# The S5 recurrence kept in PSUM, and the order of GpSimd's and ScalarE's work around it, in an encoder block on one Trainium2 core

## The chip, the core and the metric

The kernel runs on one core of a Trainium2 chip. The time is the device time of one execution in microseconds, as the median of several runs. The engines are TensorE (PE, with its weight loads as PEld), VectorE (DVE), ScalarE (ACT), GpSimd (POOL) and SyncE (SP), which here only issues DMAs. "arena" is one large tensor in SBUF that holds every buffer, "ps" is PSUM, eight banks of 512 float32 numbers in each of 128 partitions.

## What is computed

One layer of a bidirectional encoder for 512 tokens of width 1024, all in float32: a projection, a Mamba-2 branch (SSD), an S5 branch, gates, a layer norm, and a mixture of 16 experts. The change touches the S5 branch. Cut to it, the reference is:

```python
def _s5_direction(ug, a_re, a_im, log_step, b_re, b_im):
    lam = lax.complex(a_re, a_im)
    step = jnp.exp(log_step)[:, None]
    a_bar = jnp.exp(lam * step)
    b_bar = ((a_bar - 1.0) / lam)[..., None] * lax.complex(b_re, b_im)
    bu = jnp.einsum('blgk,gpk->blgp', ug.astype(jnp.complex64), b_bar)
    ...
    _, states = lax.associative_scan(combine, (a_seq, bu), axis=1)
    return states

def _s5_branch(u, ...):
    s_f = _s5_direction(ug, ..._f); s_b = flip(_s5_direction(flip(ug), ..._b))
    y = jnp.real(jnp.einsum('blgp,gkp->blgk', s_f + s_b, c))
    y = jax.nn.gelu(y + u * d_skip)
    return (y @ w_glu_a) * jax.nn.sigmoid(y @ w_glu_b)
```

## The kernel before

**Rounds.** The 48 groups of the S5 branch are packed in 24 pairs, and the pairs are worked through in six rounds of four (NQ = 6, QB = 4). A sequence of 512 is cut into 128 chunks of 4 tokens, so that a recurrence runs over 128 chunks, once forward (d = 0) and once backward (d = 1). The complex factor of the recurrence is split into modulus and phase: the input F is turned by a table of cosines and sines, a real scan with the modulus runs over it, and the result is turned back. The order is written out by hand; every wait is a semaphore.

**VectorE** does in round q: `maps(q + 1)`, the output maps `vc` of the next round (L1511 to L1515, then v_ready); `toeplitz_rows(q)` (L1641 to L1644); and `recur(q, 0)`, `recur(q, 1)` (L1648 to L1680). A recurrence reads F, which TensorE has put into PSUM banks 0 to 3, in four products with the tables (L1657 to L1660), adds them into zr and zi in SBUF (L1661, L1662, then F_read), runs eight scans, two for each pair (L1666, L1667), and turns the result into X with four products and two sums (L1673 to L1678, then X_ready).

**TensorE** does in round q: `toeplitz(q)`, 16 small products; `states(q)`, transposed input maps times U, which give F; `outputs(q - 1)`, which reads X of the round before and gives y5_ps; and three fills, each a tile of 128 x 512 of the gate projections. They are the tiles t = 2 to 4 in round 0, 5 to 7 in round 1 and so on, in the PSUM banks 4 and 7 by turns (`fill_bank`). The states wait for F_read of both directions of the round before, the outputs for X_ready. A fill waits until the one before the last has been drained (gate_copied).

**GpSimd** makes the tables. `tables(q, d)` (L529 to L535) waits for X_ready of the same direction one round before, whose tables it overwrites. `state_maps(q + 1)` (L492 to L501) makes the input maps `wc` of the next round; it stands between the two tables of round q and waits for in_ready, ScalarE's copy of the maps of the round before.

**ScalarE** does in round q: the copies of the Toeplitz products and of the four transposed maps, `gelu(q - 1)` (waits for y5_ps), `input_blocks(q + 1)` (eight copies, waits for w_ready of the state maps), and the drains of the three fills, with `output_blocks(q + 1)` behind the first. A drain is a sigmoid into the one buffer gstage and a DMA to gate_scratch; the next drain waits until that has landed.

**SyncE** stores and reloads the Toeplitz blocks and the outputs y5, and loads the projection weights in slices of 2 MB.

Of the kernel before, what the change touches and what calls it, by code (L numbers as in the profile page):

```python
# [24 lines left out]
ALU = mybir.AluOpType  # L25
# [137 lines left out]
def encoder(nc, A, out):  # L163
# [21 lines left out]
    with ExitStack() as ctx:  # L185
# [142 lines left out]
        toep_ps toep_copied toep_built toep_stored toep_loaded wT_ps wT_copied F_ps F_read par_ready conv_tap sel_built  # L328
# [176 lines left out]
        def _(pool):  # L505
# [64 lines left out]
            powers(coarse, FINE.bit_length() - 1)  # L570
            for q in range(NQ):
                for d in range(2):
                    tables(q, d)
                    pool.wait_ge(s.tab_ready, 2 * q + d + 1)
                    if d == 0 and q + 1 < NQ:
                        maps_tmp = pool_tmp.rearrange("p a b -> p (a b)").rearrange("p (i c) -> p i c", i=4)
                        state_maps(pool, n, [maps_tmp[:, i, :] for i in range(4)], q + 1)
# [28 lines left out]
        def _(act):  # L606
# [123 lines left out]
            for q in range(NQ):  # L730
                toeplitz_copied(q)
                for j in range(QB):
                    i = QB * q + j
                    act.wait_ge(s.wT_ps, i + 1)
                    if i >= 2:
                        act.wait_ge(s.F_ps, i - 1)
                    f(wT[:, i % 2].rearrange("p a b -> p (a b)"), ps[:, 5 + i % 2, :], ACT.Copy).then_inc(s.wT_copied, 1)
                if q >= 1:
                    gelu(q - 1)
                if q + 1 < NQ:  # L740
                    input_blocks(q + 1)
                for t in range(fills_before[q], fills_before[q + 1]):
                    (gate if t < GATES else first_channels)(t, fill_bank(t))
                    if t == fills_before[q] and q + 1 < NQ:
                        output_blocks(q + 1)
# [14 lines left out]
            for b in range(1, XBC // 512 + 1):  # L760
                for j in range(4):
                    i = 4 * b + j
                    if i < 20:
                        act.wait_ge(s.xbc_ps, i - 3)
                        if b == 1:
                            act.wait_ge(s.toep_loaded, 16 * 2 * T * NQ)
                            act.wait_ge(s.F_read, 2 * NQ)
                        else:
                            act.wait_ge(s.conv_done, 4 * b)
# [173 lines left out]
        def _(pe):  # L943
# [105 lines left out]
            def states(q):  # L1049
                pe.wait_ge(s.in_ready, q + 1)  # L1050
                pe.wait_ge(s.u_loaded, 16 * 2 * T)
                if q >= 1:
                    pe.wait_ge(s.F_read, 2 * q)
# [45 lines left out]
            for b in range(1, XBC // 512 + 1):  # L1099
                if b < XBC // 512:  # L1100
                    w = slice_wait()
                    for j in range(4):
                        i = 4 * b + j
                        if i == 6:
                            pe.wait_ge(s.F_read, 2 * NQ)
# [364 lines left out]
        def _(dve):  # L1470
# [175 lines left out]
            def recur(q, d):  # L1646
# [6 lines left out]
                if d == 1:  # L1653
                    F = [x[:, :, ::-1] for x in F]
                c, sn = cos_t[:, d], sin_t[:, d]
                flat = lambda x: x.rearrange("p g c -> p (g c)")
                tt(zr, F[0], c, ALU.mult)  # L1657
                tt(zi, F[1], c, ALU.mult)
                tt(t1, F[1], sn, ALU.mult)
                n.link(tt(t2, F[0], sn, ALU.mult))  # L1660
                tt(zr, zr, t1, ALU.add)  # L1661
                tt(zi, zi, t2, ALU.subtract).then_inc(s.F_read, 1)  # L1662
                dve.wait_ge(s.F_read, 2 * q + d + 1)
                for g in range(QB):
                    decay = modulus[:, d, QB * q + g:QB * q + g + 1].to_broadcast([P, NC])
                    n.done(dve.tensor_tensor_scan(t1[:, g], decay, zr[:, g], 0.0, ALU.mult, ALU.add))  # L1666
                    n.done(dve.tensor_tensor_scan(t2[:, g], decay, zi[:, g], 0.0, ALU.mult, ALU.add))  # L1667
# [5 lines left out]
                n.done(tt(o[0], e(t1), e(c), ALU.mult))  # L1673
                n.done(tt(o[1], e(t1), e(sn), ALU.mult))
                n.done(tt(zr, t2, sn, ALU.mult))
                n.link(tt(zi, t2, c, ALU.mult))
                tt(o[0], o[0], e(zr), ALU.subtract)
                ins = tt(o[1], o[1], e(zi), ALU.add)  # L1678
                ins.then_inc(s.X_ready, 1)
# [299 lines left out]
```

## Time and profile before

| | |
|---|---|
| median of 3 runs | 2209.75 us (2207.89 to 2210.27) |
| the profiled execution, its own time | 2202.2 us |
| its span | 2200.5 us |
| busy over the span | PE 1983.0 us (90%), PEld 943.1 (43%), DVE 648.4 (29%), ACT 381.4 (17%), POOL 237.3 (11%) |
| mean granted TensorE clock | 0.951 of full speed |
| 0 to 89 us | transposes, projections, the parameters of the S5 branch |
| 89 to 320 us | the six S5 rounds |
| 320 to 820 us | conv, SSD branch, gates and mixing |
| 820 us to the end | layer norm, router, experts; DMA share 0.96 |

Busy time of an engine is the time in which an instruction of it runs. The share over the span says little here, since the stages have different limits; the section after the next shows rows of the S5 rounds alone. A row of the timeline gives start, length, engine, line, operation, output and inputs with their shapes, and in brackets the idle time before it with the engine that ended it. Queued instructions overlap a little, so that a row's length can be more than the distance to the next start.

### The profile page before, as it was taken

What the parts mean: (1) busy time and instruction counts of PE and PEld (TensorE: products, weight loads), DVE (VectorE), ACT (ScalarE), POOL (GpSimd) and SP (SyncE); (2) the same over time, 40 slices, a digit from 0 to 9 for tenths busy, and PEclk for the clock granted to TensorE, in tenths of its full rate; (3) what the DMA queues carried; (4) which work ended last, traced back from release to release, by engine and by line L of the source; (5) the groups of instructions that cost most, each with busy time, mean ns of one, the idle gap of its engine ahead of it and who ended that gap; (6) DMA issues with size and microseconds to landing.
All of it is one profiled execution on the core that took longest, in us unless ns stands there. A gap on an engine that the chain in (4) does not pass through costs nothing.

```text
span 2200.5 us, 19980 instructions
## 1 busy us (share of the span) xinstructions
PE 1983.0 (90%) x8382; PEld 943.1 (43%) x8382; DVE 648.4 (29%) x1101; ACT 381.4 (17%) x684; POOL 237.3 (11%) x238
## 2 busy tenths in 40 slices
PE   8887899999989999799989888988988888988987
PEld 4555554456654445434334334333333333333332
DVE  6599977477750113400100100100100100100102
ACT  1433312257760002100001000000000000000001
POOL 1767520032210000000000000000000000000001
PEclk9898999999989999899989999999989999999989
DMA  5621222101113228699999999999999999999995
GB/s 141 125 73 64 69 58 81 67 29 45 42 58 134 86 72 353 257 421 425 427 428 428 427 427 428 427 427 428 428 426 428 428 427 426 429 426 427 429 427 225
DMA packets 88074, 625.49 MB, mean 284 GB/s; under 512 B 21180, under 2 KB 34736, under 8 KB 57776
## 3 DMA queue, kind: packets, MB, share of 16 engines
q1 hardware_dynamic: 75552, 616.41, 68.4%
q10 hardware_dynamic: 12432, 7.79, 1.2%
q8 instruction: 67, 1.10, 0.2%
q14 instruction: 23, 0.19, 0.0%
HBM read 614.39 MB, written 9.78 MB: 284 GB/s over the span
## 4 chain that ended last, share of the span: by engine, by line
PE 56%; DMA 27%; DVE 4%; ACT 1%; issue 1%; POOL 0%; SPq 0%; DVEq 0%; POOLq 0%
PE ps L945 54%; DMA arena<-in_w_e 27%; ACT arena L610 1%; DVE arena L1864 0%; DVE arena L1862 0%; DVE arena L1792 0%; PE ps L1396 0%; DVE arena L1955 0%; DVE arena L1912 0%; DVE arena L1666 0%; DVE arena L1667 0%; PE ps L1430 0%; PE ps L1120 0%; DVE arena L1753 0%; DVE arena L1949 0%
## 5 line engine op out<-in xcount | busy, mean ns | idle before, releaser
L945 PE MATMUL ps<-arena 128*64 128x512 f32 (+6 forms) x7850 | 1917.8, 529 | 186.6 <-DMA arena<-in_w_e 113.5
L945 PEld LDWEIGHTS ps<-arena 128*64 128x64 f32 (+2 forms) x7850 | 880.2, 164 | 1199.3 <-issue 1044.5
L610 ACT ACTIVATE arena<-ps 128x512 f32<-128x512 f32 (+5 forms) x292 | 164.7, 595 | 1684.5 <-PE ps L945 979.7
L1921 DVE TENSOR_TENSOR arena<-arena,ps 128x512 f32<-128x512 f32 (+1 forms) x48 | 30.2, 644 | 568.3 <-PE ps L945 568.2
L602 POOL TENSOR_TENSOR arena<-arena 128x1024 f32<-128x1024 f32 x3 | 7.1, 2351 | 1364.5 <-ACT arena L610 1364.5
L1930 DVE TENSOR_TENSOR arena<-arena,ps 128x512 f32<-128x512 f32 x48 | 33.1, 690 | 341.3 <-PE ps L945 341.3
L610 ACT ACTIVATE arena<-arena 128x128 f32<-128x128 f32 (+8 forms) x250 | 110.1, 503 | 78.2 <-DVE arena L1828 20.8
L610 ACT ACT_TABLE_LOAD x74 | 94.9, 1283 | 25.4 <-issue 23.7
L1712 DVE SCALAR_TENSOR_TENSOR arena<-arena 128x512 f32<-128x512 f32 x80 | 60.2, 753 | 2.8
L1912 DVE TENSOR_TENSOR arena<-arena 128x512 f32<-128x512 f32 x8 | 5.6, 694 | 179.2 <-PE ps L1430 179.2
L1511 DVE TENSOR_TENSOR arena<-arena 128x320 f32<-128x320 f32 x48 | 38.7, 865 | 0.4
L590 POOL TENSOR_TENSOR arena<-arena 128x768 f32<-128x768 f32 x16 | 24.4, 1524 | 101.2 <-PE ps L945 101.2
L492 POOL TENSOR_TENSOR arena<-arena 128x256 f32<-128x256 f32 x40 | 31.8, 826 | 1.1
L1667 DVE TENSOR_TENSOR_SCAN arena<-arena 128x128 f32<-128x128 f32 x48 | 31.8, 663 | 0.0
L1666 DVE TENSOR_TENSOR_SCAN arena<-arena 128x128 f32<-128x128 f32 x48 | 31.5, 655 | 0.4
L1810 DVE TENSOR_TENSOR arena<-ps,arena 128x512 f32<-128x512 f32 x8 | 5.5, 690 | 74.9 <-PE ps L945 39.1
L1818 DVE TENSOR_TENSOR arena<-ps,arena 128x512 f32<-128x512 f32 x8 | 5.5, 692 | 71.0 <-PE ps L945 71.0
L529 POOL TENSOR_TENSOR arena<-arena 128x512 f32<-128x512 f32 (+4 forms) x19 | 17.6, 926 | 67.6 <-DVE arena L1678 66.8
L591 POOL TENSOR_TENSOR arena<-arena 128x768 f32<-128x768 f32 x16 | 24.9, 1554 | 0.0
L587 POOL TENSOR_TENSOR arena<-arena 128x512 f32<-128x512 f32 x4 | 5.6, 1404 | 168.7 <-ACT arena L610 148.0
L1396 PE MATMUL ps<-arena 128*128 128x128 f32 x176 | 23.4, 289 | 0.0
L1396 PEld LDWEIGHTS ps<-arena 128*128 128x128 f32 x176 | 21.9, 211 | 3.1 <-DVE arena L1921 3.1
(192 smaller groups left out, 685.1 us busy)
## 6 DMA issues: line engine op xcount, KB each, us to landing
arena<-in_w_e SPq DMA_DIRECT2D x120, 2816.0 KB, 28.9
arena<-in_w_e SPq DMA_DIRECT2D x80, 2048.0 KB, 28.1
arena<-in_w_e SPq DMA_DIRECT2D x16, 1408.0 KB, 21.3
arena<-in_w_in SPq DMA_DIRECT2D x9, 2048.0 KB, 8.8
arena<-in_w_e SPq DMA_DIRECT2D x16, 1024.0 KB, 29.8
arena<-in_w_in SPq DMA_DIRECT2D x5, 1536.0 KB, 6.3
arena<-in_w_out_ssd SPq DMA_DIRECT2D x4, 1536.0 KB, 6.7
gate_scratch<-arena ACTq DMA_DIRECT2D x16, 256.0 KB, 2.9
```

Of the source, the lines that this page charges most:

```text
L492: n.done(eng.tensor_tensor(tmp[t], x, y, ALU.mult))
L590: pool.tensor_tensor(rhs_f, first(m_le, HG), last(da[:, c, f], P), ALU.mult)
L591: pool.tensor_tensor(rhs_b, first(m_ge, HG), last(da[:, c, b], P), ALU.mult).then_inc(s.mats_ready, 1)
L610: return act.activation(out, in_, func, **kw)
L945: return pe.matmul(out, lhsT, rhs, start=a, stop=z)
L1396: r = pe.transpose(ps[:, i, P * t:P * t + P], block[:, t, :], ident)
L1511: n.done(tt(tv[t], x, y, ALU.mult))
L1666: n.done(dve.tensor_tensor_scan(t1[:, g], decay, zr[:, g], 0.0, ALU.mult, ALU.add))
L1667: n.done(dve.tensor_tensor_scan(t2[:, g], decay, zi[:, g], 0.0, ALU.mult, ALU.add))
L1712: r = stt(cacc[:, j], raw[:, j, k:k + SEQ], conv_w[:, i, k:k + 1], cacc[:, j], ALU.mult, ALU.add)
L1921: tt(o, o, ps[:, i, 0:w], ALU.mult).then_inc(s.hid_ready, 1)
L1930: r = tt(o, o, ps[:, 6 + k % 2, :], ALU.add)
```

## The change

Four things are changed. The recurrence works in place in the PSUM banks of F: the two products with the sine go to t1 and t2 in SBUF, the rest is written over F, the scans run on F, and only X is in SBUF; F_read is gone, and what waited for it (the states, ScalarE's first copies of the conv input, the last outputs) waits for X_ready. GpSimd's backward table of round q waits for the output maps of round q + 1 (v_ready), and the state maps are made behind both tables, for round q + 2 (round 0 makes those of rounds 1 and 2). ScalarE's input blocks stand ahead of GELU.

```diff
@@ gpsimd
+            maps_tmp = pool_tmp.rearrange("p a b -> p (a b)").rearrange("p (i c) -> p i c", i=4)
             for q in range(NQ):
                 for d in range(2):
+                    if d == 1 and q + 1 < NQ:
+                        pool.wait_ge(s.v_ready, q + 2)
                     tables(q, d)
                     pool.wait_ge(s.tab_ready, 2 * q + d + 1)
-                    if d == 0 and q + 1 < NQ:
-                        maps_tmp = pool_tmp.rearrange("p a b -> p (a b)").rearrange("p (i c) -> p i c", i=4)
-                        state_maps(pool, n, [maps_tmp[:, i, :] for i in range(4)], q + 1)
+                for q_ in ([1] if q == 0 else []) + ([q + 2] if q + 2 < NQ else []):
+                    state_maps(pool, n, [maps_tmp[:, i, :] for i in range(4)], q_)
@@ scalar
+                if q + 1 < NQ:
+                    input_blocks(q + 1)
                 if q >= 1:
                     gelu(q - 1)
-                if q + 1 < NQ:
-                    input_blocks(q + 1)
...
-                            act.wait_ge(s.F_read, 2 * NQ)
+                            act.wait_ge(s.X_ready, 2 * NQ)
@@ tensor, states
                 if q >= 1:
-                    pe.wait_ge(s.F_read, 2 * q)
+                    pe.wait_ge(s.X_ready, 2 * q)
...
-                            pe.wait_ge(s.F_read, 2 * NQ)
+                            pe.wait_ge(s.X_ready, 2 * NQ)
                             outputs(NQ - 1)
@@ vector, recur
-                if d == 1:
-                    F = [x[:, :, ::-1] for x in F]
+                f_re, f_im = [x[:, :, ::-1] for x in F] if d else F
                 c, sn = cos_t[:, d], sin_t[:, d]
-                tt(zr, F[0], c, ALU.mult)
-                tt(zi, F[1], c, ALU.mult)
-                tt(t1, F[1], sn, ALU.mult)
-                n.link(tt(t2, F[0], sn, ALU.mult))
-                tt(zr, zr, t1, ALU.add)
-                tt(zi, zi, t2, ALU.subtract).then_inc(s.F_read, 1)
-                dve.wait_ge(s.F_read, 2 * q + d + 1)
+                n.done(tt(t1, f_im, sn, ALU.mult))
+                n.link(tt(t2, f_re, sn, ALU.mult))
+                n.done(tt(f_re, f_re, c, ALU.mult))
+                n.link(tt(f_im, f_im, c, ALU.mult))
+                n.done(tt(f_re, f_re, t1, ALU.add))
+                n.link(tt(f_im, f_im, t2, ALU.subtract))
                 for g in range(QB):
                     decay = modulus[:, d, QB * q + g:QB * q + g + 1].to_broadcast([P, NC])
-                    n.done(dve.tensor_tensor_scan(t1[:, g], decay, zr[:, g], 0.0, ALU.mult, ALU.add))
-                    n.done(dve.tensor_tensor_scan(t2[:, g], decay, zi[:, g], 0.0, ALU.mult, ALU.add))
+                    n.done(dve.tensor_tensor_scan(f_re[:, g], decay, f_re[:, g], 0.0, ALU.mult, ALU.add))
+                    n.done(dve.tensor_tensor_scan(f_im[:, g], decay, f_im[:, g], 0.0, ALU.mult, ALU.add))
                 n.wait()
...
-                n.done(tt(o[0], e(t1), e(c), ALU.mult))
-                n.done(tt(o[1], e(t1), e(sn), ALU.mult))
-                n.done(tt(zr, t2, sn, ALU.mult))
-                n.link(tt(zi, t2, c, ALU.mult))
-                tt(o[0], o[0], e(zr), ALU.subtract)
-                ins = tt(o[1], o[1], e(zi), ALU.add)
-                ins.then_inc(s.X_ready, 1)
+                n.done(tt(o[0], e(f_re), e(c), ALU.mult))
+                n.link(tt(o[1], e(f_re), e(sn), ALU.mult))
+                n.link(tt(f_re, f_im, sn, ALU.mult))
+                n.link(tt(f_im, f_im, c, ALU.mult))
+                n.done(tt(o[0], o[0], e(f_re), ALU.subtract))
+                tt(o[1], o[1], e(f_im), ALU.add).then_inc(s.X_ready, 1)
+                n.wait()
```

GpSimd, behind the first table of round 0, before: the state maps of round 1 (L492 to L495) and then the backward table (L529). The names in brackets are the semaphores an instruction waits for.

```order
L492 TENSOR_TENSOR arena<-arena 128x256 [waits in_ready,tab_ready,pool_step]
L492 TENSOR_TENSOR arena<-arena 128x256 x3
L494 TENSOR_TENSOR arena<-arena 128x4x64 [waits pool_step]
L495 TENSOR_TENSOR arena<-arena 128x4x64
L492 TENSOR_TENSOR arena<-arena 128x256 [waits pool_step]
L492 TENSOR_TENSOR arena<-arena 128x256 x3
L494 TENSOR_TENSOR arena<-arena 128x4x64 [waits pool_step]
L495 TENSOR_TENSOR arena<-arena 128x4x64
L529 TENSOR_TENSOR arena<-arena 128x512 [waits pool_step,w_ready]
```

The same place in the changed kernel:

```order
L529 TENSOR_TENSOR arena<-arena 128x512 [waits v_ready,tab_ready,pool_step]
L530 TENSOR_TENSOR arena<-arena 128x512
L531 TENSOR_TENSOR arena<-arena 128x512
L532 TENSOR_TENSOR arena<-arena 128x512
L534 TENSOR_TENSOR arena<-arena 128x512 [waits pool_step]
L535 TENSOR_TENSOR arena<-arena 128x512
L492 TENSOR_TENSOR arena<-arena 128x256 [waits in_ready,tab_ready,pool_step]
```

The six instructions of the backward table have moved ahead of the state maps of round 1, and its first one waits for v_ready.

VectorE, the forward recurrence of round 0, before, from the last product with F to the first of the products that make X:

```order
L1660 TENSOR_TENSOR arena<-ps,arena 128x512
L1661 TENSOR_TENSOR arena<-arena 128x512 [waits dve_step]
L1662 TENSOR_TENSOR arena<-arena 128x512
L1666 SCALAR_TENSOR_TENSOR arena<-arena 128x128 [waits F_read]
L1667 SCALAR_TENSOR_TENSOR arena<-arena 128x128
...
L1673 TENSOR_TENSOR arena<-arena 128x4x127 [waits dve_step]
```

The same place in the changed kernel (its scans are L1665 and L1666):

```order
L1659 TENSOR_TENSOR ps<-ps,arena 128x512 [waits dve_step]
L1660 TENSOR_TENSOR ps<-ps,arena 128x512
L1661 TENSOR_TENSOR ps<-ps,arena 128x512 [waits dve_step]
L1662 TENSOR_TENSOR ps<-ps,arena 128x512
L1665 SCALAR_TENSOR_TENSOR ps<-arena,ps 128x128 [waits dve_step]
L1666 SCALAR_TENSOR_TENSOR ps<-arena,ps 128x128
...
L1672 TENSOR_TENSOR arena<-ps,arena 128x4x127 [waits dve_step]
```

Sums and scans have moved from SBUF (arena) to PSUM (ps), and no instruction shown has two inputs in the arena any more.

## Rows read from the trace of the kernel before

**Rows 1.** The page, the chain that ended last, its shares by line.

```profile
PE ps L945 54%; DMA arena<-in_w_e 27%; ACT arena L610 1%; DVE arena L1864 0%; DVE arena L1862 0%; DVE arena L1792 0%; PE ps L1396 0%; DVE arena L1955 0%; DVE arena L1912 0%; DVE arena L1666 0%; DVE arena L1667 0%; PE ps L1430 0%; PE ps L1120 0%; DVE arena L1753 0%; DVE arena L1949 0%
```

**Rows 2.** The chain in order of time: start, length, what.

```profile
257.59 1.21 DVE arena L1678
...
258.85 27.19 PE ps L945 x88
```

**Rows 3.** Windows: length, busy (PE, PEld, DVE, ACT, POOL; or PE), clock, DMA share, GB/s.

```profile
123.00:126.00 3.00, 3.00 (x30) 0.50 0.22 87
136.00:177.00 41.00, 34.71 (x168) 22.38 (x168) 40.43 (x57) 13.29 (x23) 25.86 (x24) 0.92 0.26 82
177.00:184.00 7.00, 6.92 (x42) 0.73 0.00 0
295.00:320.00 25.00, 25.00 (x89) 1.00 0.09 19
```

**Rows 4.** Timeline of TensorE, rounds 0 to 5.

```profile
96.50 22.61 PE L945 MATMUL ps<-arena 128*128 128x128 f32 x64
122.61 3.45 PE L945 MATMUL ps<-arena 128*32 128x64 f32 x32 [3.49 <-ACT arena L610]
...
245.87 1.95 PE L945 MATMUL ps<-arena 128*32 128x64 f32 x32 [0.78 <-ACT arena L610]
...
258.85 27.18 PE L945 MATMUL ps<-arena 128*128 128x128 f32 x88 [4.98 <-DVE arena L1678]
286.80 1.95 PE L945 MATMUL ps<-arena 128*32 128x64 f32 x32 [0.78 <-ACT arena L610]
```

**Rows 5.** Timeline of VectorE, rounds 0 and 1.

```profile
98.55 0.69 DVE L1657 TENSOR_TENSOR arena<-ps,arena 128x512 f32<-128x512 f32 x1 [2.12 <-PE ps L945]
...
143.36 2.65 DVE L1511 TENSOR_TENSOR arena<-arena 128x320 f32<-128x320 f32 x4
...
147.03 0.25 DVE L1641 COPY arena<-arena 32x192 f32<-32x192 f32 x1
...
147.76 0.67 DVE L1657 TENSOR_TENSOR arena<-ps,arena 128x512 f32<-128x512 f32 x1
...
149.56 0.67 DVE L1660 TENSOR_TENSOR arena<-ps,arena 128x512 f32<-128x512 f32 x1
150.26 0.69 DVE L1661 TENSOR_TENSOR arena<-arena 128x512 f32<-128x512 f32 x1
...
151.59 0.43 DVE L1666 TENSOR_TENSOR_SCAN arena<-arena 128x128 f32<-128x128 f32 x1
...
158.11 0.69 DVE L1657 TENSOR_TENSOR arena<-ps,arena 128x512 f32<-128x512 f32 x1
...
161.88 1.57 DVE L1662 TENSOR_TENSOR arena<-arena 128x512 f32<-128x512 f32 x1
163.48 1.37 DVE L1666 TENSOR_TENSOR_SCAN arena<-arena 128x128 f32<-128x128 f32 x1
...
177.06 4.36 DVE L1511 TENSOR_TENSOR arena<-arena 128x320 f32<-128x320 f32 x4
```

**Rows 6.** Timeline of GpSimd, rounds 0 and 1.

```profile
90.75 1.09 POOL L529 TENSOR_TENSOR arena<-arena 128x512 f32<-128x512 f32 x1
...
97.72 2.40 POOL L492 TENSOR_TENSOR arena<-arena 128x256 f32<-128x256 f32 x4
...
158.24 1.09 POOL L529 TENSOR_TENSOR arena<-arena 128x512 f32<-128x512 f32 x1 [13.79 <-DVE arena L1678]
```

**Rows 7.** Timeline of ScalarE, rounds 0 and 5.

```profile
106.74 3.14 ACT L610 ACTIVATE arena<-arena 64x512 f32<-64x512 f32 x8 [9.43 <-POOL arena L495]
...
111.20 0.60 ACT L610 ACTIVATE arena<-ps 128x512 f32<-128x512 f32 x1
...
121.86 0.60 ACT L610 ACTIVATE arena<-ps 128x512 f32<-128x512 f32 x1 [6.09 <-DMA gate_scratch<-arena]
...
320.05 0.60 ACT L610 ACTIVATE arena<-ps 128x512 f32<-128x512 f32 x1 [6.28 <-PE ps L945]
```

More of the change, by code:

```diff
@@ L327, in encoder @@
         sin_done v_ready w_ready rot_angle rot_sin rot_ready gate_ps gate_copied g_stored sg_loaded bd_ready in_ready
-        toep_ps toep_copied toep_built toep_stored toep_loaded wT_ps wT_copied F_ps F_read par_ready conv_tap sel_built
+        toep_ps toep_copied toep_built toep_stored toep_loaded wT_ps wT_copied F_ps par_ready conv_tap sel_built
         tab_ready X_ready y5_ps y5_copied y5_stored yT5_loaded ysT_ready slice_used dve_step act_step
@@ L1652, in recur @@
                 F = [ps[:, 2 * d + r, :].rearrange("p (g c) -> p g c", g=QB) for r in range(2)]
-                if d == 1:
-                    F = [x[:, :, ::-1] for x in F]
+                f_re, f_im = [x[:, :, ::-1] for x in F] if d else F
                 c, sn = cos_t[:, d], sin_t[:, d]
-                flat = lambda x: x.rearrange("p g c -> p (g c)")
-                tt(zr, F[0], c, ALU.mult)
-                tt(zi, F[1], c, ALU.mult)
-                tt(t1, F[1], sn, ALU.mult)
-                n.link(tt(t2, F[0], sn, ALU.mult))
-                tt(zr, zr, t1, ALU.add)
-                tt(zi, zi, t2, ALU.subtract).then_inc(s.F_read, 1)
-                dve.wait_ge(s.F_read, 2 * q + d + 1)
+                n.done(tt(t1, f_im, sn, ALU.mult))
[4 more added lines that the diff above has]
+                n.link(tt(f_im, f_im, t2, ALU.subtract))
                 for g in range(QB):
                     decay = modulus[:, d, QB * q + g:QB * q + g + 1].to_broadcast([P, NC])
-                    n.done(dve.tensor_tensor_scan(t1[:, g], decay, zr[:, g], 0.0, ALU.mult, ALU.add))
-                    n.done(dve.tensor_tensor_scan(t2[:, g], decay, zi[:, g], 0.0, ALU.mult, ALU.add))
+                    n.done(dve.tensor_tensor_scan(f_re[:, g], decay, f_re[:, g], 0.0, ALU.mult, ALU.add))
+                    n.done(dve.tensor_tensor_scan(f_im[:, g], decay, f_im[:, g], 0.0, ALU.mult, ALU.add))
                 n.wait()
```

## The prediction

> **What bounds the kernel now.** I read the page first, then the stretch of the S5 rounds engine by engine. The chain that ended last is 54% matmuls and 27% loads of expert weights [rows 1]; those loads come late and start when the layers before them are done. So a microsecond taken off the chain in the S5 rounds (about 90 to 295 us) comes off the end, unless another wait takes it back. In the rounds the chain runs through VectorE: it reaches L1678, the last step of a recurrence, and only then TensorE goes on with the 88 matmuls of outputs and fills [rows 2]. In a window of one round, 41 us long, VectorE is busy for 40.43 us, TensorE for 34.71 and GpSimd for 25.86 [rows 3]. TensorE's own rows show its wait for L1678, 4.98 us at 258.85 [rows 4]. VectorE is therefore the bound.
>
> TensorE pays a second time. After the wait the granted clock of 177 to 184 us is 0.73, that is, partly the lower level (1.2 GHz) instead of 2.4 GHz; at 295 to 320 us, behind no such wait, it is 1.00 [rows 3]. How long is a round in which TensorE waits for nobody? The last one shows it: the Toeplitz products start at 286.80 [rows 4] and the last of its three fills is released to ScalarE at 320.05 [rows 7], 33.25 us; with the 0.75 us in which ScalarE drains the fill and TensorE waits for it, 34.0 us. The round before it takes 286.80 - 245.87 = 40.93 us. The difference of 6.93 us is the wait of 4.98 and some 1.95 us of low clock.
>
> **Why VectorE takes 40.9 us.** A recurrence is 20 instructions. For direction 0 of round 1, with GpSimd idle, it takes 158.11 - 147.76 = 10.35 us; for direction 1, while GpSimd works, 177.06 - 158.11 = 18.95 us; the maps take 143.36 to 147.03, 3.67 us, for a direction that is alone and about 7.1 us for one beside GpSimd [rows 5]. The slow instructions are those with both inputs in SBUF: beside GpSimd L1662 takes 1.57 us and L1666 1.37 us; alone an addition of that shape (L1661) takes 0.69 and L1666 0.43 us. The products with F from PSUM take 0.69 us at 158.11, where GpSimd's table work starts at 158.24 [rows 5, 6]. An input in PSUM is what keeps GpSimd's work from showing.
>
> **The change, part by part.** (1) The recurrence stays in PSUM. All 20 instructions remain, and each now has at most one input in SBUF. By the row at 158.11 they take what they take alone. Three more places wait for what went before. Queued instructions start 0.60 us apart (147.76 to 149.56 is three of them), one behind a wait 0.70 us after the last, so the addition is 3 x 0.10 = 0.3 us and a recurrence takes 10.7 us [rows 5]. No row has an instruction of VectorE that writes PSUM, nor a scan that reads it. Below, I see nothing that makes it faster than the 0.60 us of the uncontended rows. Above, the nearest row is the contended scan, 1.37 us for 0.43. I take the uncontended value, since reading PSUM costs nothing in the rows of the same shape (0.67 against 0.69 us).
>
> The Trainium skill (VectorE: DVE Perf Modes, section on the TRN2 errata) gives a VectorE instruction with a PSUM source 62 cycles more of fixed cost than one with an SBUF source, and its rules for authors advise to copy a matmul's output to SBUF where many operations follow. By the page, as an estimate, a recurrence would be 20 x 65 ns = 1.3 us dearer, 12.0 us. The rows at 147.76 and 150.26 show no such addition.
>
> (2) The maps run alone, because GpSimd's backward table waits until they are done: 2 x 3.67 = 7.3 us, with 0.7 us of Toeplitz rows (147.03 to 147.76) [rows 5]. VectorE's round is then 7.3 + 0.7 + 2 x 10.7 = 29.4 us. That is below TensorE's 34.0, so TensorE becomes the bound, with 4.6 us to spare. A recurrence may take 13.0 us before VectorE shows again.
>
> (3) GpSimd. A table takes 6.97 us (90.75 to 97.72) and a state map 2 x 4.0 = 8.0 us alone (a direction is four products of 2.40 us together and two sums of 0.7; from 97.72 to its release of ScalarE at 106.74 it took 9.0, half of it contended) [rows 6, 7]. Two tables and a map are 22 us of a 34 us round. The backward table now waits for the maps and lies beside the forward recurrence, which it precedes by far; what is queued behind it is a state map, needed only a round later. In steady rounds this is covered; the cover is 12 us.
>
> (4) TensorE's states now wait for X of the round before, not for the reading of F, since the scans occupy the four banks. The outputs, next in TensorE's queue, waited for the same X already. With VectorE at 29.4 us and TensorE at 34.0, X is ready some 6 us before TensorE comes to it. Cost nothing; it would cost only with VectorE as the bound, and then the 6 us of states lie beside the 8 us of maps.
>
> (5) ScalarE's input blocks stand ahead of GELU. Their 3.1 us fall before the outputs are done, where ScalarE was waiting. No gain on the path, no loss.
>
> (6) Round 0 loses. There the state map of round 1 stood directly behind the first table and now stands behind both. GpSimd starts the second table at 97.7, ends at 104.7, and the map ends at 112.7 instead of 106.7. ScalarE's input blocks waited for it, start at 106.74 [rows 7] and will start at 112.8. Queued behind them on ScalarE: the table load, the drain of fill 2 (111.20, now 117.3), the output blocks, the drains of fills 3 and 4. TensorE's fill 4 uses the bank of fill 2 and cannot start before 117.9; it would have started at 112.2, 6.9 us before its end at 119.1 [rows 4]. It idles 5.6 us; behind a gap of 3.49 us the clock was already at 0.50 [rows 3, 4], so I add the 1.9 us of low clock: 117.9 + 6.9 + 1.9 = 126.7, drained at 127.3. The Toeplitz products of round 1 start at 127.4, not at 122.61 [rows 4]. That costs 4.8 us. Bounds: without the low clock 2.9 us; with a store of the gate scratch that lands late in front of the last drain (before, ScalarE waited for one until 121.86 [rows 7]) 7.5 us.
>
> **The sum.** From the Toeplitz products of round 1 to those of round 5 it is now 286.80 - 122.61 = 164.2 us, and will be 4 x 34.0 = 136.0: 28.2 us less. Round 0 takes 4.8 back. 28.2 - 4.8 = 23.4 us. What follows (conv, SSD, mixing, experts) is released by TensorE's progress, and VectorE and GpSimd stand no later against it than before. Against the profiled execution, whose own time is 2202.2 us, this is 2178.8. The median of the runs shown is 7.5 us above that execution; 2209.75 - 23.4 = 2186.3 us. The bounds of round 0 give 2184.4 to 2189.0, and with 0.5 us of a round either way 2183 to 2191 for this case.
>
> **Rivals.** (A) Relief in part, 2198 us: instructions that write PSUM, or scans on it, take more than the 2.3 us a recurrence has to spare. At 14.5 us a recurrence VectorE's round is 8.0 + 29.0 = 37.0, and the gain is 23.4 - 4 x 3.0 = 11.4. For it: no row shows such a write. Against: it needs 0.19 us more on each of 20 instructions. A loss of the same size further down would look alike in the time.
>
> (B) No relief, 2214 us: GpSimd slows the instructions in PSUM as well, so the change does not do what it says. Before, 17 us of GpSimd's work lengthened one recurrence by 8.6 us, 0.5 us each. With 22 us of it in a round VectorE has 29.4 + 11 = 40.4, the round of today, and the round-0 loss of 4 to 5 us stays. Against: the 0.69 us at 158.11.
>
> The Trainium skill (SBUF — State Buffer, section Who interferes with whom) says that a VectorE instruction with at most one SBUF input does not contend with GpSimd outside the two-port modes, and one with two does when GpSimd reads SBUF. The rows of L1657 and L1662 agree (0.69 and 1.57 us); that it holds for scans on PSUM, only the page says.
>
> (C) Slower, from the scans: a running sum that is read from and written to the same PSUM bank costs what a contended scan costs, 1.37 us instead of 0.32 from start to start. Eight of them are 8.4 us, a recurrence 19.1. VectorE would start at 98.6, finish round 0 at 136.8 (98.6 is its first start [rows 5]) and come out of four rounds of 46.2 at 321.6; the states behind that take 6 us more and end near 327.7, where they now end near 294.8 (286.80 plus 1.95 of Toeplitz products and 6.0 of states). That is 33 us, 2243 us. It decides from 15.8 us a recurrence (98.6 + 2R + 4(8.0 + 2R) + 6.1 = 294.8), a scan of 0.95 us. Only here does the new wait of the states bite, since VectorE and TensorE then take turns.
>
> **Chances.** Forecast 0.76, A 0.13, B 0.06, C 0.05. The likeliest case has 2186.3 us with 2183 to 2191; to leave no more than two in ten outside, the range goes on towards A, to 2197. A measurement of this kernel can tell about 0.2%, 4.4 us, from no change. The forecast and A lie beyond that: faster 0.89. B straddles the bound: same 0.03; the rest of B and C make slower 0.08.
>
> **What would show it.** The L1657 rows and all behind them at 0.6 to 0.7 us whatever GpSimd does; recurrences of 10.7 us in both directions; maps of 7.3 us with GpSimd idle; no wait of TensorE for the recurrence after round 0; Toeplitz products 34.0 us apart, near 127.4, 161, 195, 229 and 263; ScalarE waiting for GpSimd until about 112.7 in round 0. It is wrong if VectorE's scans are longer than 0.6 us, if TensorE still waits for the last line of the recurrence in rounds 2 to 4, or if the first Toeplitz start is later than 130.

## The result, and the profile after

The changed kernel takes 2181.95 us (median of 4 runs, 2179.34 to 2182.37), beside 2210.01 us for the kernel before (4 runs, 2207.89 to 2210.27; three of them are those shown ahead of the prediction). The ratio is 0.9873, 95% interval 0.9856 to 0.989: 28 us less, and 1 us below the range of the prediction. Its profiled execution has an own time of 2182.37 us, a span of 2180.5 us and a mean granted clock of 0.952.

The page of the changed kernel, busy time over the span and the chain that ended last by line:

```profile
PE 1980.1 (91%) x8382; PEld 938.9 (43%) x8382; DVE 601.0 (28%) x1101; ACT 381.4 (17%) x684; POOL 217.7 (10%) x238
...
PE ps L947 59%; DMA arena<-in_w_e 28%; ACT arena L612 1%; PE ps L1062 0%; DVE arena L1863 0%; DVE arena L1861 0%; DVE arena L1791 0%; DVE arena L1954 0%; DVE arena L1911 0%; ACT L612 0%; POOL arena L492 0%; PE ps L1432 0%; PE ps L1122 0%; DVE arena L1752 0%; DVE arena L1948 0%
```

VectorE is busy 47.4 us less and GpSimd 19.6 us less, for the same work: that is what contention had cost. The lines of the recurrence are no longer among those that the page lists, as they were before [rows 1]; GpSimd's L492, the state maps that are made in round 0, has come in.

Timeline of TensorE, the last fill of round 0 and the starts of rounds 1, 2 and 5 (start, length, engine, line, operation, in brackets the idle time before and what ended it):

```profile
119.73 9.72 PE L947 MATMUL ps<-arena 128*128 128x512 f32 x16 [6.00 <-ACT arena L612]
130.23 1.95 PE L947 MATMUL ps<-arena 128*32 128x64 f32 x32 [0.78 <-ACT arena L612]
...
164.08 1.95 PE L947 MATMUL ps<-arena 128*32 128x64 f32 x32 [0.78 <-ACT arena L612]
...
265.63 1.95 PE L947 MATMUL ps<-arena 128*32 128x64 f32 x32 [0.78 <-ACT arena L612]
```

The waits of TensorE in rounds 1 to 4, in total, their number and the longest, and the window of the same stretch (length, busy PE, PEld, DVE, ACT, POOL, clock, DMA share, GB/s):

```profile
PE ps L947 <- ACT arena L612: 4.9, 9, 0.8
```

```profile
130.23:265.63 135.40, 131.27 (x673) 82.72 (x674) 118.67 (x215) 53.20 (x92) 85.84 (x92) 1.00 0.26 83
```

A round is 33.85 us, four of them 135.4 us where they were 164.2 [rows 4]. In these four rounds TensorE no longer waits for VectorE at all, and its clock is 1.00 throughout, where a round of before had 0.92 [rows 3]. Round 0 shows the loss: 6.00 us of idle time in front of its last fill. (The whole S5 stretch starts 2.1 us later in this execution, as GpSimd's first table shows below; the prediction's own positions are tested in the next section.)

Timeline of VectorE in round 1: a scan and a sum in PSUM, the second recurrence, the maps and the Toeplitz rows.

```profile
138.26 0.69 DVE L1657 TENSOR_TENSOR arena<-ps,arena 128x512 f32<-128x512 f32 x1 [0.74 <-PE ps L947]
...
140.92 0.70 DVE L1661 TENSOR_TENSOR ps<-ps,arena 128x512 f32<-128x512 f32 x1
...
142.59 0.40 DVE L1666 TENSOR_TENSOR_SCAN ps<-arena,ps 128x128 f32<-128x128 f32 x1
142.90 0.40 DVE L1665 TENSOR_TENSOR_SCAN ps<-arena,ps 128x128 f32<-128x128 f32 x1
...
149.05 0.69 DVE L1657 TENSOR_TENSOR arena<-ps,arena 128x512 f32<-128x512 f32 x1
...
159.82 1.70 DVE L1513 TENSOR_TENSOR arena<-arena 128x320 f32<-128x320 f32 x4
...
164.63 0.49 DVE L1517 SCALAR_TENSOR_TENSOR arena<-arena 128x320 f32<-128x320 f32 x1
166.85 0.73 DVE L1643 COPY arena<-arena 32x192 f32<-32x192 f32 x1 [1.74 <-ACT arena L612]
...
169.70 1.31 DVE L1646 TENSOR_TENSOR arena<-arena 32x64 f32<-32x64 f32 x1
172.11 0.69 DVE L1657 TENSOR_TENSOR arena<-ps,arena 128x512 f32<-128x512 f32 x1 [1.10 <-PE ps L947]
```

Timeline of GpSimd: the first table of round 0, state maps beside the recurrence of round 1, the table that waited for the maps.

```profile
92.84 1.09 POOL L529 TENSOR_TENSOR arena<-arena 128x512 f32<-128x512 f32 x1
...
142.27 2.40 POOL L492 TENSOR_TENSOR arena<-arena 128x256 f32<-128x256 f32 x4
...
165.34 1.09 POOL L529 TENSOR_TENSOR arena<-arena 128x512 f32<-128x512 f32 x1 [8.32 <-DVE arena L1517]
```

A recurrence takes 149.05 - 138.26 = 10.79 us and the second 10.77 us, though GpSimd works beside the first (state maps from 142.27). The maps take 159.82 to 165.12, 5.3 us. VectorE then waits 1.74 us for ScalarE and 1.10 us for TensorE: it has become the engine that waits. The four Toeplitz rows, now beside GpSimd's table, take 166.85 to 171.01, 4.2 us for what took 0.7 [rows 5].

### The profile page after: what moved, and what is told of

Its sections match the earlier page's. It is cut to its first block, busy times and chain, and to the rows that moved or that the text cites. A ratio compares the mean times of both kernels' runs of the same rounds, so it can differ in the third digit from the quotient of the medians.

```text
span 2180.5 us, 19987 instructions
## 1 busy us (share of the span) xinstructions
PE 1980.1 (91%) x8382; PEld 938.9 (43%) x8382; DVE 601.0 (28%) x1101; ACT 381.4 (17%) x684; POOL 217.7 (10%) x238
## 4 chain that ended last, share of the span: by engine, by line
PE 60%; DMA 28%; DVE 3%; ACT 2%; issue 1%; POOL 1%; SPq 0%; DVEq 0%; POOLq 0%
PE ps L947 59%; DMA arena<-in_w_e 28%; ACT arena L612 1%; PE ps L1062 0%; DVE arena L1863 0%; DVE arena L1861 0%; DVE arena L1791 0%; DVE arena L1954 0%; DVE arena L1911 0%; ACT L612 0%; POOL arena L492 0%; PE ps L1432 0%; PE ps L1122 0%; DVE arena L1752 0%; DVE arena L1948 0%
## 5 line engine op out<-in xcount | busy, mean ns | idle before, releaser
L1920 DVE TENSOR_TENSOR arena<-arena,ps 128x512 f32<-128x512 f32 (+1 forms) x48 | 30.2, 644 | 575.3 <-PE ps L947 575.3
L1513 DVE TENSOR_TENSOR arena<-arena 128x320 f32<-128x320 f32 x48 | 28.6, 658 | 0.6
L492 POOL TENSOR_TENSOR arena<-arena 128x256 f32<-128x256 f32 x40 | 24.9, 656 | 8.1 <-ACT arena L612 7.4
L1398 PE MATMUL ps<-arena 128*128 128x128 f32 x176 | 23.4, 289 | 0.0
L1708 DVE TENSOR_SCALAR arena<-arena 128x512 f32<-128x512 f32 x20 | 10.9, 546 | 38.1 <-ACT arena L612 38.1
L529 POOL TENSOR_TENSOR arena<-arena 128x512 f32<-128x512 f32 (+4 forms) x19 | 16.9, 888 | 44.8 <-DVE arena L1517 26.9
L1931 DVE SCALAR_TENSOR_TENSOR arena<-arena,ps 128x512 f32<-128x512 f32 x8 | 5.5, 690 | 54.9 <-PE ps L947 54.9
```

The lines of the kernel that those rows point to most:

```text
L492: n.done(eng.tensor_tensor(tmp[t], x, y, ALU.mult))
L529: n.done(pool.tensor_tensor(out[0], x[0], y[0], ALU.mult))
L1398: r = pe.transpose(ps[:, i, P * t:P * t + P], block[:, t, :], ident)
L1513: n.done(tt(tv[t], x, y, ALU.mult))
L1708: r = ts(cacc[:, j], raw[:, j, 0:SEQ], conv_w[:, i, 0:1], conv_b[:, i:i + 1], ALU.mult, ALU.add)
L1920: tt(o, o, ps[:, i, 0:w], ALU.mult).then_inc(s.hid_ready, 1)
```

## The experiments

### Both kernels again

Both kernels without an edit, for a second profiled execution of each.

> The kernel before, unchanged, to see a second profiled execution of it: the one on which the prediction rests took 2202.2 us, the median is 2210. Theory 1 (the missing gain is not in the S5 rounds): from the Toeplitz products of round 1 to those of round 5 it again takes 164.2 us, the start of round 1 is within 2 us of 122.6 plus the shift of GpSimd's first table, and if the execution takes 2208 to 2210 us, the 6 to 8 us more lie in the expert part (from the first expert matmul at 915.0 to the end it took 1285.5). Theory 2 (it is in the rounds): the rounds take 168 to 172 us in an execution of 2210 us, because waits there vary. Time expected by both: 2208 to 2211 us, ratio 1.000.

Measured: 2205.19 us (10 runs, 2203.62 to 2210.52), ratio 1.0001 [0.9989, 1.0012] to 19 further runs of the same kernel at 2207.26 (2202.79 to 2210.62). The profiled execution that the prediction starts from, 2202.2 us, lies below every one of these. This profiled execution took 2205.25 us and not 2208 to 2210, so that it can't decide between the theories; its four rounds take 164.4 us and its expert part 1286.7 us, 1.2 us more than in the first profile.

> The changed kernel, unchanged, for a second profiled execution on the same chip. Both theories: 2180 to 2183 us, rounds 33.85 us apart (135.4 us for four), and the expert part from its first matmul to the end within 2 us of 1287.0. If the expert part differs by 5 us or more between two executions of the same kernel, theory 1 has its mechanism.

Measured: 2180.94 us (4 runs, 2178.91 to 2183.11), 0.9884 [0.9864, 0.9904]: 25.6 us less, between 21 and 30. GpSimd's first table starts at 90.75 us, as before [rows 6]. Timelines of ScalarE and TensorE of this execution:

```profile
112.53 3.14 ACT L612 ACTIVATE arena<-arena 64x512 f32<-64x512 f32 x8 [14.40 <-POOL arena L495]
```

```profile
117.63 8.83 PE L947 MATMUL ps<-arena 128*128 128x512 f32 x16 [4.55 <-ACT arena L612]
127.24 1.95 PE L947 MATMUL ps<-arena 128*32 128x64 f32 x32 [0.78 <-ACT arena L612]
...
262.63 1.95 PE L947 MATMUL ps<-arena 128*32 128x64 f32 x32 [0.78 <-ACT arena L612]
```

The prediction had ScalarE's input blocks at 112.8, the last fill at 117.9 and 6.9 + 1.9 = 8.8 us long, the Toeplitz products at 127.4 and 263. All are hit within 0.4 us; only the idle time in front of the last fill is 4.55 us, not 5.6. Round 5 starts 286.80 - 262.63 = 24.2 us earlier than in the profile of before; 23.4 was the forecast. The expert part takes 1286.8 us, as expected, so that it doesn't hold the rest of the gain.

### One part alone

The new recurrence, with X_ready in the places of F_read, but GpSimd and ScalarE in the order of before:

```diff
@@ gpsimd, against the changed kernel
-                    if d == 1 and q + 1 < NQ:
-                        pool.wait_ge(s.v_ready, q + 2)
                     tables(q, d)
...
-                for q_ in ([1] if q == 0 else []) + ([q + 2] if q + 2 < NQ else []):
-                    state_maps(..., q_)
+                    if d == 0 and q + 1 < NQ:
+                        state_maps(..., q + 1)
@@ scalar
-                input_blocks(q + 1); gelu(q - 1)
+                gelu(q - 1); input_blocks(q + 1)
```

> The recurrence in PSUM with its waits alone; GpSimd's order and ScalarE's order as before. By the prediction's own terms: no loss in round 0 (the state map of round 1 still stands between the two tables, Toeplitz products of round 1 near 122.6 to 124); maps beside GpSimd again, 10.9 instead of 7.3 us, so VectorE has 10.9 + 0.8 to 2.5 + 21.5 = 33 to 35 us a round against 34.0 of TensorE. Theory order-not-needed: TensorE stays the bound, 34 us a round, gain 27 to 29 us, 4 to 5 us faster than the changed kernel. Theory order-needed: the maps make VectorE the bound, rounds of 36 us or more, gain under 20 us.

Measured: 2185.16 us (2180.55 to 2190.27), 0.9907 [0.9884, 0.993]. TensorE, the starts of rounds 1, 2 and 5 and two waits for X:

```profile
121.09 3.46 PE L945 MATMUL ps<-arena 128*32 128x64 f32 x32 [2.43 <-ACT arena L610]
156.45 1.95 PE L945 MATMUL ps<-arena 128*32 128x64 f32 x32 [0.78 <-ACT arena L610]
...
195.00 1.06 PE L1060 MATMUL ps<-arena 128*128 128x128 f32 x8 [1.75 <-DVE arena L1675]
...
262.57 1.95 PE L945 MATMUL ps<-arena 128*32 128x64 f32 x32 [0.78 <-ACT arena L610]
266.25 1.07 PE L1060 MATMUL ps<-arena 128*128 128x128 f32 x8 [1.73 <-DVE arena L1675]
```

VectorE, the four products of one direction of the maps, beside GpSimd's table:

```profile
164.01 4.78 DVE L1511 TENSOR_TENSOR arena<-arena 128x320 f32<-128x320 f32 x4
```

Neither theory had this: the rounds, 34.9 to 35.7 us, lie between the 34 of the one and the 36 of the other, and so does the gain of 20.5 us (15 to 26 by the interval).

The reverse, the new order with the recurrence in SBUF:

```diff
@@ gpsimd and scalar, against the kernel before
+                    if d == 1 and q + 1 < NQ:
+                        pool.wait_ge(s.v_ready, q + 2)
                     tables(q, d)
...
+                for q_ in ([1] if q == 0 else []) + ([q + 2] if q + 2 < NQ else []):
+                    state_maps(..., q_)
...
-                gelu(q - 1); input_blocks(q + 1)
+                input_blocks(q + 1); gelu(q - 1)
```

> GpSimd's and ScalarE's new order alone; the recurrence in SBUF as before. By the prediction: maps alone (7.3 us), but both recurrences beside GpSimd's 22 us of work, 0.5 us longer for each: 8 + 20.7 + 11 = 39.7 us a round against 40.9, and round 0 loses 4.8 us: 2205 to 2215 us, no change that can be told. Rival: contention costs more per us of GpSimd's work when all of it meets two-input instructions, rounds of 42 us or more and 2218 us or slower.

Measured: 2200.8 us (2198.04 to 2204.6), 0.9973 [0.9962, 0.9984], 6 us less, where no change that can be told was expected. Its rounds are 33.8 to 39.3 us, 149.2 us for four where 164.2 were and 159 had been expected, but from GpSimd's first table to the start of round 1 it takes 40.6 us instead of 31.9. A sum of two SBUF tiles still takes VectorE 1.66 us:

```profile
152.59 1.66 DVE L1663 TENSOR_TENSOR arena<-arena 128x512 f32<-128x512 f32 x1
```

Keeping the recurrence in PSUM is nearly the whole gain. Beside it the new order pays for itself only in the rounds: with it they are 33.85 us, without it 34.9 to 35.7, where the maps are slowed (4.78 us above for 1.70) and the states wait up to 1.75 us for L1675; that is 6.1 us over four rounds. But it starts round 1 at 127.24 instead of 121.09, also 6.1 us. At round 5 both stand at the same point, 262.57 and 262.63. What separates them in the profiles lies behind it: from there to the first expert matmul 634.3 us pass in this one and 630.9 in the changed kernel. That the medians differ by 4.2 us for another reason is not excluded; the rounds don't show one.

### The loss of round 0

Two kernels take it away; their code is shortened here. In the first, GpSimd makes the state map of round 1 between the tables of round 0, as before; in the second, VectorE makes it, behind the maps of round 1:

```diff
@@ gpsimd, first kernel
                     pool.wait_ge(s.tab_ready, 2 * q + d + 1)
+                    if q == 0 and d == 0:
+                        state_maps(pool, ..., 1)
-                for q_ in ([1] if q == 0 else []) + ([q + 2] if q + 2 < NQ else []):
-                    state_maps(pool, ..., q_)
+                if q + 2 < NQ:
+                    state_maps(pool, ..., q + 2)
@@ vector, second kernel (round 1's map is not made by GpSimd)
                     maps(q + 1)
                 if q == 0:
+                    state_maps(dve, ..., 1)
```

> The changed kernel, with the state map of round 1 put back between the two tables of round 0; later rounds as changed. Tests term 6 of the prediction (round 0 loses 4.8 us). Theory round-0 (the term is right): ScalarE's input blocks start near 106 instead of 112.8, TensorE's fill 4 does not wait, the Toeplitz products of round 1 start at 121 to 123 instead of 127.2 (first table at 90.75), and the kernel is 4 to 5 us faster than the changed one: 2176 to 2177 us. Rival (the loss is hidden or given back): the backward table comes 7 us later, VectorE's round 1 slips, TensorE waits 4 us or more for L1677 in round 1 or 2, and the time is that of the changed kernel, 2180 to 2182 us.

Measured: 2178.67 us (2175.41 to 2179.85), 0.9869 [0.9854, 0.9883]. ScalarE's input blocks and its last drain of round 0, and TensorE's start of round 1, in an execution whose first table starts at 91.83:

```profile
106.72 3.14 ACT L614 ACTIVATE arena<-arena 64x512 f32<-64x512 f32 x8 [9.07 <-POOL arena L495]
...
121.52 0.60 ACT L614 ACTIVATE arena<-ps 128x512 f32<-128x512 f32 x1 [6.22 <-DMA gate_scratch<-arena]
```

```profile
122.26 3.28 PE L949 MATMUL ps<-arena 128*32 128x64 f32 x32 [2.80 <-ACT arena L614]
157.44 1.95 PE L949 MATMUL ps<-arena 128*32 128x64 f32 x32 [0.78 <-ACT arena L614]
```

The input blocks are back where they were [rows 7], and counted from GpSimd's first table round 1 begins 6.1 us earlier than in the second profile of the changed kernel. 1.3 us of this go at once: the Toeplitz products behind the wait take 3.28 us instead of 1.95, and the first round 35.18 us instead of 33.85. Against the changed kernel's 0.9873 and 0.9884 the ratio is 1 to 3 us better, where 4 to 5 us had been expected, and the intervals meet: the rows show the step, the times do not tell its size.

> The changed kernel, with the state map of round 1 made by VectorE, which waits for ScalarE from 81.8 to 89.2 us; GpSimd goes on with round 2. Theory round-0: input blocks start behind the copies of the transposed maps (near 98), round 1 starts at 120 to 122.6 (now held by the landing of the gate stores), 5 to 7 us faster than the changed kernel: 2174 to 2176 us. Rival: VectorE's work beside GpSimd's powers delays the first table by 1 to 2 us, past the end of the states at 98.5, and takes that much back, 2176 to 2178 us.

Measured: 2176.89 us (2173.35 to 2178.69), 0.9861 [0.9845, 0.9877], the fastest kernel of the study. TensorE's start of round 1, and the window behind it:

```profile
119.46 1.95 PE L947 MATMUL ps<-arena 128*32 128x64 f32 x32 [0.78 <-ACT arena L612]
```

```profile
122.00:126.00 4.00, 3.75 (x34) 3.51 (x32) 3.90 (x10) 2.07 (x5) 0.00 (x0) 1.00 0.00 0
```

Here TensorE meets neither the long wait nor the lower clock. The place of the round-0 loss is shown by both. Its worth is less sure: round 5 starts at 254.86, 10.8 us earlier than in the first profile of the changed kernel and 7.8 earlier than in the second (10.6 and 9.7 with the starts of GpSimd's first table aligned), and the ratio is lower than the changed kernel's two by only 0.0012 and 0.0023, 3 to 5 us, with intervals that meet. The time of 2176.89 us lies where the rival was expected, but the rows don't bear the rival out: GpSimd's first table starts at 92.69, no later than in the first profile of the changed kernel, and round 1 starts before the 120 to 122.6 us that the other theory had.

### Two parts of the change taken back

The code is shortened:

```diff
@@ scalar, first kernel, against the changed kernel
-                input_blocks(q + 1); gelu(q - 1)
+                gelu(q - 1); input_blocks(q + 1)
@@ gpsimd, second kernel
-                    if d == 1 and q + 1 < NQ:
-                        pool.wait_ge(s.v_ready, q + 2)
                     tables(q, d)
```

> The changed kernel with GELU ahead of the input blocks, as before. By term 5 of the prediction the order on ScalarE has no place on the path: rounds 33.85 us apart, 2180 to 2182 us. Rival: the state maps two rounds ahead wait for ScalarE's input blocks (in_ready); put back by 5 to 6 us, GpSimd's map and next forward table reach into the maps of VectorE and lengthen them by 1 to 3 us; it would show in the time only if VectorE used up its 4.6 us: 2182 to 2186 us.

ScalarE has GELU ahead of the input blocks again, the rest is the changed kernel. Measured: 2182.58 us (2178.11 to 2184.99), 0.9888 [0.9866, 0.9909], rounds of 33.85 us.

> The changed kernel without GpSimd's wait for the output maps: the backward table runs beside VectorE's maps. By the prediction's terms the maps take 10.9 instead of 7.3 us, VectorE's round 33 us, just under TensorE's 33.85: no change, 2180 to 2183 us, rounds 33.9 us apart. Rival: the wait is needed, VectorE comes too late by 1 to 2 us a round and TensorE waits for L1677: 2184 to 2190 us.

GpSimd's two lines with v_ready are left out. Measured: 2180.45 us (2179.51 to 2183.86), 0.9882 [0.9867, 0.9896], again 33.85 us a round. VectorE's maps take 10.8 us beside GpSimd's table, as expected. Neither kernel differs from the changed kernel's 0.9884. As the old order as a whole has rounds of 34.9 to 35.7 us, the part of the new order that helps the rounds is by elimination the place of the state maps, behind both tables and two rounds ahead; it was not tested alone.

### How much longer a recurrence may be

Products that are not needed are linked into each recurrence, with an input in PSUM:

```diff
                 n.link(tt(f_im, f_im, t2, ALU.subtract))
+                for _ in range(3):      # 6 in the second kernel
+                    n.link(tt(zr, f_re, c, ALU.mult))
```

> The changed kernel with three more products of VectorE in each recurrence (PSUM times a table into a buffer that is not read), 0.73 us each, 2.2 us a recurrence, 12.98 us in all. Work is added, the result is untouched. Forecast's account (VectorE's round is 8.0 + 2R, bound at 13.0 us): no change, 2181 us, rounds 33.9 us. Account from the changed kernel's trace (maps 5.3 us but Toeplitz rows 4.1 us beside GpSimd, so 9.5 + 2R, bound at 12.2 us): rounds of 35.3 to 35.7 us, TensorE waits 1 to 2 us for L1677, 5 to 8 us slower than the changed kernel, 2186 to 2189 us.

> The same with six more products in a recurrence, 4.4 us, 15.2 us in all. Work is added, the result is untouched. Forecast's account: rounds of 38.4 us, 18 us slower than the changed kernel, 2199 us. Account from the trace: rounds of 39.9 us, 24 us slower, 2205 us. Rival (the scans or the PSUM accesses have slack of their own and the added ones hide): under 10 us slower.

Measured: with three 2186.28 us (2185.23 to 2187.0), 0.9902 [0.9887, 0.9917]; with six 2205.59 (2204.59 to 2207.24), 0.9998 [0.9988, 1.0007], the time of the kernel before. Timeline of VectorE with three, from one recurrence to that of the next round:

```profile
172.92 0.67 DVE L1657 TENSOR_TENSOR arena<-ps,arena 128x512 f32<-128x512 f32 x1
...
176.89 2.15 DVE L1664 TENSOR_TENSOR arena<-ps,arena 128x512 f32<-128x512 f32 x3
...
198.83 1.70 DVE L1513 TENSOR_TENSOR arena<-arena 128x320 f32<-128x320 f32 x4
...
207.56 0.67 DVE L1657 TENSOR_TENSOR arena<-ps,arena 128x512 f32<-128x512 f32 x1
```

Timeline of TensorE with six:

```profile
202.81 1.95 PE L947 MATMUL ps<-arena 128*32 128x64 f32 x32 [0.78 <-ACT arena L612]
208.17 1.94 PE L1062 MATMUL ps<-arena 128*128 128x128 f32 x8 [3.42 <-DVE arena L1679]
```

With three, VectorE has no idle time left: two recurrences in 198.83 - 172.92 = 25.91 us and 8.73 us for maps and rows make a round of 34.64. TensorE's 33.85 is reached at (33.85 - 8.73) / 2 = 12.56 us a recurrence. The changed kernel, at 10.78 us, has 1.8 us to spare in each. (Its idle time of 2.8 us a round would give 1.4; but there all four Toeplitz rows lie beside GpSimd's table, here the first takes 0.25 us.) The time with three is the expected one in part by luck: the rounds are 34.64 us, not 35.3 to 35.7, TensorE waits for X three times for at most 1.0 us, and the four rounds grow by 2.6 us of the 5.3 by which the medians differ. With six (15.1 us a recurrence) VectorE's round is 39.0 us, TensorE waits 3.3 to 5.6 us for X in front of each round's states, and from 161.67 to 281.05 a round takes 39.8 us. The gain is gone: the states and VectorE now take turns in part, as rival C described.

### The kernel before, profiled twice more

> The kernel before, unchanged, for a third profiled execution. Its two profiled executions so far took 2202.2 and 2205.3 us, while the median of its runs is 2207 to 2208 and the highest 2210.6. Theory clock (the spread comes from low-clock spells of TensorE behind short waits outside the rounds, and from the start): an execution of 2207 us or more has a round 1 to round 5 of 164.2 to 164.4 us all the same, and 1.5 to 6 us more from the Toeplitz products of round 5 to the first expert matmul (628.2 us in the fastest). Theory rounds: the stretch of the rounds itself is 2 us or more longer.

> The same again, for a fourth profiled execution; the same expectations. If its time lies near 2203, the stretch from round 5 to the first expert matmul is near 628 us, and if it lies near 2209, near 632 to 634 us.

Both are the kernel before without an edit. Measured: 2204.7 us (2202.47 to 2209.54) and 2206.34 (2203.33 to 2211.52), ratios 0.9993 and 0.9994, beside 25 runs at 2206.7. The profiled execution of the second has 2210.48 us. Windows of this one, from the last Toeplitz start to the first expert matmul and two stretches in it:

```profile
288.50:920.70 632.20, 599.17 (x1991) 327.61 (x1991) 312.38 (x535) 211.88 (x385) 62.56 (x46) 0.96 0.26 98
352.00:366.00 14.00, 10.41 (x29) 5.42 (x28) 11.85 (x18) 7.40 (x12) 0.00 (x0) 0.76 0.44 151
...
476.50:492.50 16.00, 14.07 (x51) 8.80 (x50) 12.07 (x20) 10.19 (x20) 4.85 (x4) 0.89 0.00 1
```

The same stretches in the execution of 2202.2 us from which the prediction started:

```profile
286.80:915.00 628.20, 596.05 (x1989) 326.42 (x1989) 313.06 (x536) 211.88 (x385) 63.36 (x47) 0.97 0.26 98
350.00:364.00 14.00, 11.00 (x35) 6.07 (x34) 11.88 (x17) 7.40 (x12) 0.00 (x0) 0.88 0.43 151
...
474.80:490.80 16.00, 15.22 (x60) 9.79 (x61) 12.92 (x22) 8.33 (x15) 4.26 (x3) 1.00 0.01 1
```

The first of the two is the faster one (2203.91 us) and takes 627.9 us from round 5 to the first expert matmul, as expected; the second takes 632.2 us, also as expected, but the rounds of both, 164.9 and 165.4 us, are a little above the 164.2 to 164.4 of theory clock.

The slower execution loses 8.3 us against the faster one, in small pieces: 0.5 before the rounds (round 1 starts at 123.09), 1.2 in the four rounds (165.4 us), 4.0 from there to the experts, 1.8 in the experts (1287.3 against 1285.5) and 0.8 around the span. Of the 4.0 us, 3.1 are longer matmuls, 599.17 us busy for 596.05, and the clock is lower in single stretches of 14 to 16 us. It is one and the same kernel whose matmuls meet the lower clock more or less often.

## Why the prediction was wrong by a little, and where it was right

**The bound, and its relief: right.** The recurrence takes 10.78 us in both directions (10.7 was said) and TensorE waits for no recurrence. Rival A fell with this recurrence, B and C with the scan of 0.40 us beside GpSimd's state maps. Of the two rules of the Trainium skill weighed there, that of VectorE: DVE Perf Modes (section on the TRN2 errata) would have given 12.0 us a recurrence, by the estimate made from it; the rows do not bear it out, 0.67 to 0.70 us an instruction of 512 columns with its input, or its input and output, in PSUM. The rule of the Trainium skill in SBUF — State Buffer (section Who interferes with whom), that outside the two-port modes an instruction of VectorE with at most one SBUF input does not contend with GpSimd, is borne out for scans on PSUM too, 0.40 us beside GpSimd as without it.

**Maps and rows: two terms off, of opposite sign.** Said: 7.3 + 0.7 = 8.0 us. Measured: 5.3 + 4.2 = 9.5 us. The rows of one direction "alone" in the kernel before were not alone (four products took 2.65 us there and take 1.70 in the changed kernel), and the Toeplitz rows now lie beside the backward table. VectorE has 2.8 us to spare in a round instead of 4.6, which does not show. The bound of 13.0 us a recurrence is 12.6 by the kernel with three added products.

**The round of 34.0 us: right**, 33.85.

**The new waits: right that they cost nothing.** The states' wait for X shows only where VectorE's round is longer than TensorE's: with the added products, and up to 1.75 us with the order of before. Without v_ready nothing changes, and GELU's place is worth nothing that can be measured.

**Round 0: right.** 4.8 us were said, 127.24 - 122.61 = 4.6 came, through the steps named (input blocks, last fill, low clock). But that is a net of two terms, and the prediction had only one. From GpSimd's first table to the start of round 1 the four profiled executions of the kernel before take 31.2 to 31.9 us, the changed kernel 36.5 and 37.4, and the kernel with the recurrence in PSUM and the order of before 30.2. So the moved state map costs 6.3 us or more, and 1 to 1.7 us come back from the rest of the change. That the net agrees so closely is in part luck.

**What failed is the last step of the sum**, "The median of the runs shown is 7.5 us above that execution; 2209.75 - 23.4 = 2186.3 us". It took the median of three runs as the base, supposed with it that the changed kernel's runs would lie 7.5 us above the execution that was worked out, and gave this no range. That execution (2202.2 us) was faster than every other execution of the kernel before that was timed for this study (the next is 2202.47). Its expert part, 1285.5 us, is the shortest of all profiled executions, 1286.7 to 1287.3 us in three others of the kernel before. The median of the three runs lay above the medians of the larger sets (2206.7 to 2208.0 us over 51 runs). With 2207.3, the median of 19 runs, the same step gives 2183.9 us, in the range and 2 to 3 us above what was measured. So of the 4 to 5 us by which 2186.3 was too high, some 2.5 lie in the base.

The comparison on record, read alone, says otherwise: there the kernel before took 2210.01 us again, mostly by the same runs, and the whole miss is in the difference, 28 us for 23.4. The larger sets and the rows speak against that. From GpSimd's first table to the start of round 5 the kernel before takes 196.1, 196.2, 196.1 and 196.6 us in its four profiled executions, the changed kernel 172.8 and 171.9: 23.3 to 24.8 us less. The forecast's 23.4 lies within that.

**What stays open** is the rest of 2 us or more: the ratios give 25.6 us (21 to 30) and 28 us (24 to 32), the rows 24. The changed kernel's two profiled executions (2182.37 and 2183.11 us) were the slowest of their four runs, so that part of the rest may lie in runs of which there is no trace. The stretch from round 5 to the first expert matmul takes 627.8 and 630.9 us in the changed kernel, 627.9 to 632.2 in four executions of the kernel before, and tells no gain. The intervals do not exclude that there is no rest at all.

## What to carry to other kernels

Where VectorE's instructions with two SBUF inputs are slowed by GpSimd, keep what TensorE has written in PSUM and work on it in place: here that alone was worth 20 to 22 us of 2207 (interval 15 to 26); a new order of GpSimd's work was worth 6 us alone and, by the rows, nothing on top. Cost a reordering in its first round too: there the work moved back was waited for, and what four steady rounds gave (6.1 us) the first took. And carry no difference between one profiled execution and a median from one kernel to the next; take its size as the range of the result.

## What the runs showed of the hardware

- In-place instructions on PSUM, 128 x 512: 0.70 us, as in SBUF alone (0.69). Scans of 128 columns on PSUM: 0.40 us (0.43 behind a wait), beside GpSimd as without it. In the rounds of all nine profiled executions with the recurrence in PSUM none takes longer, while with two inputs in SBUF such instructions took up to 1.76 us, such scans up to 1.43.
- Small instructions of VectorE are slowed most beside GpSimd: a copy of 32 x 192, though it has only one input in SBUF, takes 0.25 us alone and 0.7 to 1.2 beside a table, a sum of 32 x 64 0.21 and up to 1.32, four products of 128 x 320 1.70 us alone and up to 5.3. GpSimd pays too: a product of a table (128 x 512) takes 1.09 us, up to 1.36 beside the maps and up to 1.55 beside the recurrence in SBUF.
- The 630 us between the S5 rounds and the experts take 627.9 to 632.2 us in four executions of one and the same kernel; in the two compared above, a stretch of 14 us has a granted clock of 0.76 in the one and 0.88 in the other. This spread of 4.3 us is not far from what the new order alone gave, and it is why single profiled executions could not rank the variants.
